# Half of the down-projection units of the second block computed with seven quarter products, with their weight and data sums in fp32

## The reference, cut to what matters

```python
h = rms_norm(x, g_ffn[l])
x = x + jnp.square(jax.nn.relu(h @ w_ff1[l])) @ w_ff2[l]     # w_ff1 1024 x 4096, w_ff2 4096 x 1024
```

## Time and profile before

| | |
|---|---|
| median of 3 runs | 1963.39 us (1962.83 to 1964.98) |
| the profiled execution's own time | 1964.91 us |
| its span | 1963.1 us |
| TensorE busy | 1931.0 us, 98% |
| VectorE, ScalarE, GpSimd busy | 1146.5, 767.9, 1010.7 us |
| mean granted TensorE clock | 0.994 |

### The profile page before, as it was taken

One profiled execution on the slowest core, in us unless ns is written; L12 is line 12 of the kernel. 1 busy time (PEld: TensorE's weight loads), 2 busy tenths in 40 slices (PEclk: granted clock), 3 DMA queues, 4 the chain that ended last, 5 costly groups with the idle time before them and its releaser, 6 DMA issues.

```text
span 1963.1 us, 24980 instructions
## 1 busy us (share of the span) xinstructions
PE 1931.0 (98%) x9110; PEld 1602.8 (82%) x9110; DVE 1146.5 (58%) x2009; ACT 767.9 (39%) x1142; POOL 1010.7 (51%) x1273
## 2 busy tenths in 40 slices
PE   9999999999999999999999999999999999999998
PEld 7788788888888887888888888888878888888887
DVE  7986778968766667554232325666676553233335
ACT  6444544445335555233232323344554233223232
POOL 6353374343643436666654646533447566464644
PEclk9999999999999999999999999999999999999999
DMA  5222122221221213232323232222222222323231
GB/s 196 84 76 83 56 92 93 82 86 44 100 105 65 86 65 108 87 108 86 109 90 105 88 108 86 86 86 83 87 73 102 92 102 86 108 86 107 86 108 64
DMA packets 29657, 178.92 MB, mean 91 GB/s; under 512 B 3936, under 2 KB 6112, under 8 KB 9184
## 3 DMA queue, kind: packets, MB, share of 16 engines
q1 hardware_dynamic: 27376, 173.42, 24.8%
q10 hardware_dynamic: 2160, 3.91, 0.7%
HBM read 175.22 MB, written 2.10 MB: 90 GB/s over the span
## 4 chain that ended last, share of the span: by engine, by line
PE 75%; DVE 13%; issue 5%; ACT 4%; POOL 2%; DMA 0%; SPq 0%; POOLq 0%; DVEq 0%; ACTq 0%
PE bank L584 69%; PE bank L605 2%; DVE bank L1943 2%; POOL W_lo L550 1%; DVE PR L1862 1%; PE bank L635 1%; PE bank L647 1%; DVE Y_lo L1755 1%; DVE PT_lo L1755 1%; ACT PR L1265 1%; ACT W_hi L1231 1%; ACT PT_hi L1235 1%; PE bank L846 1%; DVE PR L1883 1%; PE bank L616 1%
## 5 line engine op out<-in xcount | busy, mean ns | idle before, releaser
L550 POOL TENSOR_TENSOR W_lo<-W_raw,W_hi 128x256 fp32r<-128x256 f32 (+1 forms) x1228 | 984.9, 839 | 913.9 <-ACT W_hi L1231 913.9
L584 PE MATMUL bank<-H_hi,W_hi 128*128 128x512 f32 x1264 | 500.6, 396 | 1.6 <-DVE PRE L1995 0.9
L584 PE MATMUL bank<-H_hi,W_lo 128*128 128x512 f32 x1264 | 493.5, 390 | 0.0
L584 PE MATMUL bank<-H_lo,W_hi 128*128 128x512 f32 x1264 | 492.8, 390 | 0.0
L584 PE MATMUL bank<-Y_hi,W_hi 128*128 128x512 f32 (+1 forms) x980 | 385.2, 393 | 3.7 <-DVE Y_lo L1755 2.1
L584 PE MATMUL bank<-Y_lo,W_hi 128*128 128x512 f32 (+1 forms) x980 | 381.2, 389 | 0.0
L584 PE MATMUL bank<-Y_hi,W_lo 128*128 128x512 f32 (+1 forms) x980 | 380.9, 389 | 0.0
L1231 ACT ACTIVATE W_hi<-W_raw 128x2048 fp32r<-128x2048 f32 (+2 forms) x159 | 295.7, 1862 | 202.8 <-DMA W_raw<-in_stream 198.1
L584 PEld LDWEIGHTS bank<-H_hi,W_hi 128*128 128x128 f32 x1264 | 238.1, 188 | 50.7 <-DVE Y_lo L2321 1.8
L584 PEld LDWEIGHTS bank<-H_hi,W_lo 128*128 128x128 f32 x1264 | 237.6, 188 | 50.8
L584 PEld LDWEIGHTS bank<-H_lo,W_hi 128*128 128x128 f32 x1264 | 238.2, 188 | 47.5
(11 more groups left out here) (319 smaller groups left out, 2326.1 us busy)
## 6 DMA issues: line engine op xcount, KB each, us to landing
W_raw<-in_stream SPq DMA_DIRECT2D x159, 1024.0 KB, 4.8
out<-GT SPq DMA_DIRECT2D x8, 256.0 KB, 2.7
BT<-in_bias ACTq DMA_DIRECT2D x6, 320.0 KB, 3.0
X<-in_x SPq DMA_DIRECT2D x3, 512.0 KB, 7.8
W_raw<-in_stream SPq DMA_DIRECT2D x4, 256.0 KB, 7.5
BT<-in_rope ACTq DMA_DIRECT2D x2, 512.0 KB, 3.5
BT<-in_bias SPq DMA_DIRECT2D x2, 320.0 KB, 12.5
X<-in_x SPq DMA_DIRECT2D x2, 256.0 KB, 4.4
```

The source lines that it names most:

```text
L550: ins = nc.gpsimd.tensor_tensor(W[1][:, s, part], W_raw[:, s, part], W[0][:, s, part].bitcast(F32), ALU.subtract)
L584: mm = pe.matmul(out, lhs[a], rhs[b], start=(not begun and k == 0 and a == 0 and b == 0), stop=(not more and k == n - 1 and a == 1), skip_ ...
```

## The change

Units 42 to 45 and 50 to 53 of each layer (the down units of the second and of the third group; 16 units in all) are computed in another way. A unit is a product of a weight block of 1024 by 256 with data of 1024 by 512. Both are halved in both directions, and the eight quarter products are replaced by seven, of sums of quarters (a Winograd form). Each product is 4 tiles by 3 matmuls of 256 columns: 84 matmuls of 256 columns for a unit in place of 48 of 512.

- VectorE forms the sums in fp32: for each such unit four weight sums of 512 columns (`weight_sums`; one of them is written over the raw weights), and for the group's data, in the up part before it (`up_seven`), one sum in each of chunks 0 to 3 and three in each of chunks 4 to 7. It also makes the low parts of two of the weight sums (`sums_lo`). GpSimd makes the third in two instructions more.
- ScalarE rounds the unit's weights in two instructions after the sums (`prep_seven`), the three sums in two more (`prep_sums`), and in the up part before it the squares and the data sums; it copies three partial results from bank to bank in each unit.
- The weight sums of a group's first unit stand behind chunk 3 of the up part on VectorE, their roundings behind chunk 4 and 5 on ScalarE, the low parts of the sums behind chunk 6 on VectorE. Those of each next unit stand in the unit before it.
- VectorE adds the products straight to X. So that this needs no row factor, X is divided by RB once (down of the first group, `RBI`) and multiplied by it in the last down part.

In the diff, `seven` is TensorE's; the first `up_seven` and `down_seven` are ScalarE's, `weight_sums` and the `up_seven` and `down_seven` behind it VectorE's.

```diff
+            def seven(k, f):
...
+                def product(name, bank, lhs, rhs, ready, begun):
+                    for kt, w in enumerate(weights(lhs)):
+                        if m == 0:
+                            pe.wait_ge(b2.lo.sem, b2.lo.at(l, ready(kt), combos_of(f - 1)))
+                        mm = three(pe, bank[:, 0:256], [(w, data(rhs, kt))], begun=begun or kt > 0, more=True)
+                    mm.then_inc(b2.done.sem, 1)
...
+                if m == 0:
+                    pe.wait_ge(b2.aux.sem, b2.aux.at(l, "u6", *group(f - 1)))
+                pe.wait_ge(w_lo, low_at(n - EARLY, True))
+                received("1")
+                product("1", G[0], "a11", "b11", lambda kt: f"b{kt}", False)
+                received("7")
+                product("7", SC[0], "s3", "t3", lambda kt: f"x{4 + kt}", False)
+                copied("1")
+                pe.wait_ge(s_lo, 2 * q + 1)
+                product("6", SC[1], "s2", "t2", lambda kt: f"y{4 + kt}", True)
+                pe.wait_ge(w_lo, low_at(n - EARLY))
+                product("2", G[0], "a12", "b21", lambda kt: f"b{4 + kt}", True)
+                copied("2")
+                pe.wait_ge(s_lo, 2 * q + 2)
+                product("5", TB[0], "s1", "t1", lambda kt: f"b{4 + kt}", True)
+                product("4", SC[1], "a22", "t4", lambda kt: f"b{4 + kt}", True)
+                copied("4")
+                pe.wait_ge(s_last, q + 1)
+                product("3", TB[0], "s4", "b22", lambda kt: f"b{4 + kt}", True)
...
+            def up_seven(k, f):
...
+                for n in range(KT):
+                    if n % 2 == 0 and n < 6:
+                        prep(2, l, k + n // 2)
+                    act.wait_ge(b2.done.sem, b2.done.at(l, f"u{n}", seg, i))
...
+                    nc.scalar.activation(TMP[:, n % 2, :], G[n % 2][:, :], ACT.Relu) \
...
+                    else:
+                        act.wait_ge(b2.pre.sem, b2.pre.at(l, f"x{n}", cs))
+                        hi(b2, l, f"x{n}", Y[0][:, n - 4, 256:512], Y_raw[:, n - 4, 256:512], cs)
+                        act.wait_ge(b2.pre.sem, b2.pre.at(l, f"t{n}", cs))
+                        hi(b2, l, f"y{n}", YX[0][:, 1:3, n - 4, :], YX_raw[:, 1:3, n - 4, :], cs)
+                        hi(b2, l, f"b{n}", Y[0][:, n, :], Y_raw[:, n, :], cs)
+                    if n == 4:
+                        prep_seven(k + 3)
+                    if n == 5:
+                        prep_sums(k + 3)
...
+            def down_seven(f):
...
+                    copy("1", "1", SC[1], G[0], "2")
+                    copy("2", "6", TB[0], SC[1], "3")
+                    if m < 3:
+                        prep_seven(k + 1)
+                    copy("4", "5", TB[1], TB[0], "4")
+                    if m < 3:
+                        prep_sums(k + 1)
+                    if m == 2:
+                        prep(2, l, k + 2)
...
+            def weight_sums(k):
...
+                dve.wait_ge(*raw_landed(n))
+                dve.wait_ge(*own.last(0))
+                nc.vector.tensor_tensor(s1, a21, a22, ALU.add).then_inc(dve_step, own.step())
+                minus(a21, a11, a21)
+                minus(s2, s1, a11)
+                minus(s4, a12, s2, s_sums, q + 1)
...
+            def up_seven(f):
...
+                    nc.vector.tensor_tensor(Y_raw[:, n, :], TMP[:, n % 2, :], TMP[:, n % 2, :], ALU.mult) \
+                        .then_inc(b2.pre.sem, own.event(b2.pre, l, f"u{n}", cs))
+                    if n < 4:
+                        minus(T1_raw[:, n, :], Y_raw[:, n, second], Y_raw[:, n, first],
+                              b2.pre.sem, b2.pre.at(l, f"t{n}", cs))
+                        lo(b2, l, f"b{n}", Y[1][:, n, first], Y_raw[:, n, first], Y[0][:, n, first], cs, behind=0)
+                        lo(b2, l, f"t{n}", YX[1][:, 0, n, :], T1_raw[:, n, :], YX[0][:, 0, n, :], cs)
+                        if n == 3:
+                            weight_sums(42 + 8 * f)
+                        continue
+                    k = n - 4
+                    minus(Y_raw[:, k, second], Y_raw[:, n, second], Y_raw[:, k, second],
+                          b2.pre.sem, b2.pre.at(l, f"x{n}", cs))
+                    minus(YX_raw[:, 1, k, :], Y_raw[:, n, second], T1_raw[:, k, :])
+                    minus(YX_raw[:, 2, k, :], Y_raw[:, n, first], YX_raw[:, 1, k, :],
+                          b2.pre.sem, b2.pre.at(l, f"t{n}", cs))
+                    lo(b2, l, f"x{n}", Y[1][:, k, second], Y_raw[:, k, second], Y[0][:, k, second], cs, behind=0)
+                    lo(b2, l, f"y{n}", YX[1][:, 1:3, k, :], YX_raw[:, 1:3, k, :], YX[0][:, 1:3, k, :], cs)
+                    lo(b2, l, f"b{n}", Y[1][:, n, :], Y_raw[:, n, :], Y[0][:, n, :], cs)
+                    if n == 6:
+                        sums_lo(42 + 8 * f)
...
+            def down_seven(f):
...
+                    if m < 3:
+                        weight_sums(k + 1)
...
+                    receive_sum("7", b2.done, f"p{m}7", b.rearrange("p (a n) -> p a n", a=2), both)
+                    receive_sum("1", b2.done, f"p{m}2", a[:, first], G[0][:, 0:256])
+                    receive_sum("4", b2.aux, f"c{m}4", b[:, second], TB[1][:, 0:256])
+                    receive_sum("2", b2.done, f"p{m}4", b[:, first], SC[1][:, 0:256])
+                    if m < 3:
+                        sums_lo(k + 1)
+                    receive_sum("3", b2.done, f"p{m}3", a[:, second], TB[0][:, 0:256])
```

More of the change, by code:

```diff
@@ L70 @@
 WARMING = 13
+PRODUCTS = "1762543"
+SEVEN = {42 + 8 * i + m: (i + 1, m) for i in range(2) for m in range(4)}
 class Count:
@@ L284, in last_pair @@
         return [{"g12": "pl0", "g13": "pl1"}.get(name, name) for name in names]
+    products = [f"p{m}{k}" for m in range(4) for k in PRODUCTS]
+    receipts = [f"r{m}{k}" for m in range(4) for k in "71423"]
+    copies = [f"c{m}{k}" for m in range(4) for k in "124"]
+    combos = [f"{c}{n}" for n in range(KT) for c in ("bt" if n < 4 else "xyb")]
+    raws = [f"{c}{n}" for n in range(KT) for c in ("ut" if n < 4 else "uxt")]
     b2.done = Count(sem("proj_done2"), 1, [("", 1, lats + pools[:2]), ("h0", 1, pair_chunks),
@@ L553, in low_part, with low_half @@
                     ins.then_inc(w_lo, 1)
+        def low_half(s, h):
+            for kt in range(4 * h, 4 * h + 4):
+                part = slice(256 * kt, 256 * kt + 256)
+                ins = nc.gpsimd.tensor_tensor(W[1][:, s, part], W_raw[:, s, part],
+                                              W[0][:, s, part].bitcast(F32), ALU.subtract)
+            return ins
         for n in range(EARLY):
@@ L1163, in up @@
                         three(pe, G[0][:, :], pairs[KT - 1:], begun=True).then_inc(b2.done.sem, 1)
+                    elif seg == "fs" and n == 0:
+                        by_halves(G[0], 2, l, first, pairs).then_inc(b2.done.sem, 1)
                     else:
@@ new lines, in down_seven, with copy @@
+            def down_seven(f):
+                seg, i = group(f)
+                for m in range(4):
+                    k = 34 + 8 * f + m
+                    def copy(name, product, out, in_, back):
+                        act.wait_ge(b2.done.sem, b2.done.at(l, f"p{m}{product}", seg, i))
+                        if m:
+                            act.wait_ge(b2.free.sem, b2.free.at(l, f"r{m - 1}{back}", seg, i))
+                        elif f == 2:
+                            act.wait_ge(b2.free.sem, b2.free.at(l, "r33", *group(1)))
+                        act.wait_ge(*own.last(1))
+                        nc.scalar.activation(out[:, 0:256], in_[:, 0:256], ACT.Copy) \
+                            .then_inc(b2.aux.sem, own.event(b2.aux, l, f"c{m}{name}", seg, i))
+                    copy("1", "1", SC[1], G[0], "2")
[7 more added lines that the diff above has]
+                        prep(2, l, k + 2)
@@ new lines, in down_seven, with receive_sum @@
+            def down_seven(f):
+                seg, i = group(f)
+                first, second = token_half(0), token_half(1)
+                for m in range(4):
+                    k = 34 + 8 * f + m
+                    def receive_sum(name, count, event, out, in_):
+                        dve.wait_ge(count.sem, count.at(l, event, seg, i))
+                        dve.wait_ge(*own.last(0))
+                        nc.vector.tensor_tensor(out, out, in_, ALU.add) \
+                            .then_inc(b2.free.sem, own.event(b2.free, l, f"r{m}{name}", seg, i))
+                    if m < 3:
+                        weight_sums(k + 1)
+                    a, b = X[:, 2 * m, :], X[:, 2 * m + 1, :]
+                    both = SC[0][:, 0:256].rearrange("p (a n) -> p a n", a=1).broadcast_to([P, 2, 256])
+                    receive_sum("7", b2.done, f"p{m}7", b.rearrange("p (a n) -> p a n", a=2), both)
[5 more added lines that the diff above has]
+                    receive_sum("3", b2.done, f"p{m}3", a[:, second], TB[0][:, 0:256])
@@ L2629, in down @@
```

(20 more changed lines are left out.)

195 lines of the change are left out of this document (161 added, 34 removed).

## The result

The changed kernel takes **1994.3 us** (median of 4 runs, 1991.6 to 1994.7) against 1964.0 for the kernel before on the same chip (1962.8 to 1965.0): ratio 1.0153, 95% interval 1.0141 to 1.0165. It is slower by 30.3 us; the forecast was 1990.5, with 1975 to 2003 as its range. The profiled execution is the fastest of the four, 1991.6, with a span of 1989.8.

What follows compares the result with a forecast made beforehand. TensorE, 98% busy, was taken as the bound. Profiled execution 1964.9 us plus 24.1 (37.0 of pauses minus 12.9 saved) plus 3 for the clock gave 1992, so a median of 1990.5; range 1975 to 2003.

Steps and rivals of the forecast that it cites:

- step 1: Up part: weight sums slow GpSimd, so TensorE pauses 1.6 us for unit 41 and 0.2 at unit 40.
- matmuls saved: TensorE: 84 matmuls at 0.120 us against 48 at 0.2267 save 0.80 us a unit, 12.9 in all.
- step 5: First seven-product unit: TensorE waits 0.15 us at product 1, 1.0 and 4.9 in product 7, 0.7 before product 6.
- x6: Data sum needed by the third tile of product 7: TensorE pauses 1.0 us for it.
- x7: Data sum needed by the fourth tile of product 7: TensorE pauses 4.9 us for it.
- copy 1: Bank copy that product 6 needs, behind chunk 7's roundings on ScalarE: TensorE pauses 0.7 us.
- step 6: Next units: little slack between sums, roundings, GpSimd's first half and product 1; pauses of 0.2, 0.3 and 0.2 us.
- half clock behind x7: After each long pause TensorE's granted clock falls to half once: 0.7 us each, 3 us in all.
- Steps 2 to 4: Chunks 4 to 7: VectorE's differences and ScalarE's roundings delay relus; chunk 5's done at 16.4 us, last low part 31.9.
- the sides seldom meet: Rival: VectorE and GpSimd don't hold each other up; pauses 12.5 us against 12.9 saved, 1963 us; chance 0.06.
- Locked ports: Rival: VectorE and GpSimd lock ports for whole instructions, a pair takes 1.39 us; 2037 us; chance 0.03.
- Faster: Rival: VectorE catches up before chunk 6, a part's pauses stay under 3.2 us; 1957.7 us; chance 0.06.

Runs made afterwards that it cites:

- kernel 2: Changed kernel with GpSimd's subtractions for units 39 to 53 and the third weight sums replaced by memsets to zero; 1963.7 us, ratio 1.0003.
- kernel 1: Kernel before the change, with its 16 down units made in halves of 256 columns, 96 matmuls for 48; 1971.7 us, ratio 1.0044.
- Kernel 3: Changed kernel with the weights of units 40 and 41 (and 48, 49) rounded one chunk sooner on ScalarE; 1982.3 us, ratio 1.0098.
- kernel 4: Kernel 3 with ScalarE's first-unit weight roundings moved behind chunk 5's relu and the sums' roundings ahead of chunk 6's relu; 1976.8 us, ratio 1.0073.
- kernel 6: Kernel 4 with the square in the two up parts moved from VectorE to ScalarE; 1972.5 us, ratio 1.0043.
- kernel 9: Kernel 7 with both roundings of the next unit's weights again before the copy of product 5; 1965.7 us, ratio 1.0010.
- Kernel 8: Changed kernel with 36 matmuls of 256 columns into an unused bank before the fourth tile of product 7; 1991.1 us, ratio 1.0137.
- kernel 7: Kernel 6 plus earlier roundings of units 39 to 41, later fourth weight sum, first-unit roundings spread out, product 5's copy between next-unit roundings; 1967.0 us, ratio 1.0012.
- kernel 5: Changed kernel with the first unit's weight sums, their roundings and low parts put back two chunks later; 1992.5 us, ratio 1.0143.

## Why the prediction was right

The forecast of +27 us of work (24.1 of pauses and matmuls, 3 of clock) stands against 29.1 on the stages. For one part, in us of TensorE, a mean over the four; a pause is the distance from start to start less that of two matmuls in a row:

| step, for one part | predicted | measured |
|---|---|---|
| up part: units 40, 41 late (step 1) | 1.8 | 1.93 |
| matmuls saved | -3.2 | -3.8 |
| product 1 waits (step 5) | 0.15 | 0 |
| x6 (step 5) | 1.0 | 0.77 |
| x7 (steps 2 to 5) | 4.9 | 4.71 |
| copy 1 (step 5) | 0.7 | 0.21 |
| low halves of the next units (step 6) | 0.76 | 0.29 |
| copy 4, next units | none | 0.78 |
| half clock behind x7; second matmul after each pause | 0.75 | 2.36 |
| sum | 6.9 | 7.3 |

The matmuls saved are 43.52 - 4 x 9.93, from the units of kernel 2 that wait for nothing (kernel 1's 0.1191 gives 3.5). In the last row about 0.4 are second matmuls after pauses at full clock, 0.10 each, and the rest is half clock.

That the sums lie 0.4 apart is in part luck. The terms that were too dear (the matmuls' price, x6, x7, copy 1, the low halves, product 1) come to 2.1 us a part, those too cheap or missing (half clock and second matmuls, copy 4, the up part) to 2.5. The causes and places of the large terms, x7 and the up part, are what was foreseen.

- **Slips in the recorded sums.** Four weight sums of 1.14 from 4.8 end at 9.4, not at 9.1; measured are 9.1, since the first took 0.73. From x6 at 27.0 the fourth tile is wanted at 27.4, so x7 at 32.1 makes a pause of 4.7, not 4.9; measured are 4.71. 16 x 0.80 is 12.8.
- **Step 1** came out as written: raw weights ready at 1002.10, 5.0 after u3 (predicted 4.8), GpSimd's eight in 8.27 (8.2), ended at 12.6 (12.5). Kernel 3 takes this pause away, and 7.7 us of its 12.0 are the up parts.
- **Steps 2 to 4**, counted from the end of u3's matmuls at 997.1: relu of u5 done at 16.5 (16.4), u6's at 23.0 (23.6), x7's low part at 31.7 (31.9). Each of the moves in kernels 4 and 6 that takes work from between these relus takes it from the pause before x7: 1.16 and 1.04 us.
- **The turns of VectorE and GpSimd** are shown as the cause of the loss by kernel 2, with the small limit told there. Their price held (1.15 for 1.14, 0.85 for 0.88). The rival "the sides seldom meet" gave 1963 for no price; with no price it is 1963.7. It fell because they do meet.
- **Step 6** had the right place and the wrong instruction. It checked GpSimd against the 10.08 us of a unit, and not VectorE and ScalarE, whose loop through copy 4 is 10.99. This is the term that was missing: 0.78 a part, 3.1 us in all. In kernel 9, where the start costs less, the loop takes 2.1 of the 3.8 saved.
- **The clock.** One fall to half (1.2 GHz) in each of the four parts, as predicted. TensorE works 3.6 to 5.0 us at half clock behind x7 (in the first part from 1028.81 to 1032.45), and that stretches the matmuls by about 1.9 us, not 0.75. Little of this is a loss. Kernel 8 keeps the full clock, and its four down parts (48.88, 48.90, 48.91, 48.44) add up to only 0.3 less. In kernels 7 and 9 a part with a fall is longer by 44.93 - 44.20 = 0.7, which is my term for one fall; the waits behind it take the rest back. In kernel 2, where no later unit waits, nothing takes it back: its parts with a fall are 0.8 to 1.3 longer than the one without.
- **Copy 1** was 0.21 because TensorE ran at half speed ahead of it; where the clock stays full (kernels 7 to 9) it is 0.46, which was the bank copy I had to guess: 0.37 from bank to bank, the lower end of my two.
- **The median** is 3.8 us above the forecast, the profiled execution within 1 of the 1992 forecast for it. I took before's distance between profiled run and median (-1.5) for after's; it was +2.7. How many half-clock stretches the first block has in an execution differs from run to run, and I had no term for that.
- **Rivals.** Locked ports (2037) fell with the 1.15. "Faster" needed pauses under 3.2 us a part. The best arrangement tried has 4.5 (44.2 - 39.7) against 3.8 to be saved.

Two things stay open. No run tried to shorten the loop itself, by fewer sums in it or another engine for one of them. And no run removed the 2.3 us that the start of a part still costs in kernel 9; without them, and with the loop as it is, the four units there would take some 41.9 us by my estimate, 1.6 less than the 43.52 of before.

## What to carry to other kernels

A form with fewer matmul columns is worth only what the engines that prepare its operands can supply: here 3.8 us for each part on TensorE were set against 37 more VectorE instructions in it (53 for 16). Of the 18 among them that form or split weight sums, 13 in the first part stand beside a GpSimd that makes them take 1.6 times as long. Before such a change, write the lists of the supplying engines on one clock, with the price of a meeting for both sides, and add up two things: what the start of a run of such units costs, and the closed loop of one steady unit. A steady unit that is held at 10.99 gains nothing on the 10.88 it replaces, so in a long run of them no order of the start could pay. In a run of four, as here, two are held, and the loop leaves some 1.6 us, which the start must not use up. Listing the same work sooner on the same engine moves the pause to what is queued behind it (kernel 5).
